# Modulation weights of a diffusion backbone split into two transfers, with both layers written out

## The reference, cut to what matters

```python
mod = jnp.dot(jax.nn.silu(cvec), lp['ada_w']) + lp['ada_b']
sh1, sc1, g1, sh2, sc2, g2 = jnp.split(mod[:, None, :], 6, axis=-1)
h = rmsnorm(x, lp['norm1']) * (1 + sc1) + sh1
proj = jnp.dot(h, lp['w_in'])
q, k, v, xbc, z, dt_raw = jnp.split(proj, SPLITS, axis=-1)
...
x = x + g1 * jnp.dot(jnp.concatenate([attn, ssm], axis=-1), lp['w_out'])
h2 = rmsnorm(x, lp['norm2']) * (1 + sc2) + sh2
x = x + g2 * expert_choice_ffn(h2, lp['w_router'], lp['w_gate'], lp['w_up'], lp['w_down'])
```

## Time and profile before

| | |
|---|---|
| median of 3 runs | 2241.47 us (2241.06 to 2242.45) |
| profiled execution, its own time | 2239.1 us |
| its span, first to last instruction | 2237.4 us |
| PE busy in the span | 1940.9 us (87%) |
| DVE, ACT, POOL busy | 674.2, 306.5, 195.6 us |
| mean granted TensorE clock | 0.914 of full |
| pieces of modulation weights | 16 of 3072 KB, 26.3 us from issue to landing |

### The profile page before, as it was taken

How to read it: one execution, slowest core, us unless ns; L and a number is a source line. 1 busy time by engine, 2 the same in 40 slices (tenths; PEclk the granted TensorE clock), 3 DMA queues, 4 the chain that set the end, 5 groups by cost and what they waited for, 6 DMA issues and landing times.

```text
span 2237.4 us, 36021 instructions
## 1 busy us (share of the span) xinstructions
PE 1940.9 (87%) x15142; PEld 962.6 (43%) x15142; DVE 674.2 (30%) x1486; ACT 306.5 (14%) x684; POOL 195.6 (9%) x266
## 2 busy tenths in 40 slices
PE   2699777996699999999847997779958999999997
PEld 0265465544243443444403744645442443443443
DVE  1130675614211221121212326665251211221121
ACT  1120122301100000000012201233011000000000
POOL 0002220000000100110000022100000100100110
PEclk9899877997799999999968998679968999999998
DMA  9900101033499999999598001012226999999994
GB/s 372 412 1 1 38 1 55 7 154 122 172 384 394 396 407 406 401 409 407 195 394 340 1 0 38 1 55 80 100 104 232 387 406 398 398 409 404 399 405 132
DMA packets 54674, 526.60 MB, mean 235 GB/s; under 512 B 11790, under 2 KB 13438, under 8 KB 25886
## 3 DMA queue, kind: packets, MB, share of 16 engines
q1 hardware_dynamic: 39886, 482.29, 52.9%
q0 software_dynamic: 6336, 21.63, 4.0%
q10 hardware_dynamic: 8384, 21.76, 2.6%
HBM read 503.91 MB, written 24.38 MB: 236 GB/s over the span
## 4 chain that ended last, share of the span: by engine, by line
PE 64%; issue 23%; DMA 6%; POOL 3%; DVE 2%; SPq 1%; ACT 1%; DVEq 0%; POOLq 0%; ACTq 0%
PE PS L469 30%; PE PS L549 13%; DMA arena<-ada_w 6%; PE PS L493 5%; PE PS L495 5%; PE PS L498 4%; PE PS L795 1%; PE PS L479 1%; PE PS L457 1%; PE PS L443 1%; PE PS L519 1%; POOL RB L1536 1%; POOL RB L1545 1%; PE PS L499 1%; SPq L369 1%
## 5 line engine op out<-in xcount | busy, mean ns | idle before, releaser
L469 PE MATMUL PS<-arena,xe 128*32 128x512 f32 x6144 | 674.1, 599 | 4.0 <-DVE xe L1108 4.0
L469 PEld LDWEIGHTS PS<-arena,xe 128*32 128x32 f32 x6144 | 196.8, 111 | 457.7 <-issue 457.7
L493 PE MATMUL PS<-arena,hdT 128*32 128x512 f32 x1536 | 268.3, 599 | 3.8 <-DVE RA L1132 1.9
L495 PE MATMUL PS<-arena,hdT 128*32 128x256 f32 x1024 | 266.2, 383 | 0.0
L1119 DVE TENSOR_TENSOR RA<-RA,PS 96x512 f32<-96x512 f32 (+2 forms) x96 | 63.2, 684 | 649.7 <-ACT RA L864 646.9
L549 PE MATMUL PS<-arena,RB 128*128 128x512 f32 (+2 forms) x640 | 190.1, 456 | 0.0
L498 PE MATMUL PS<-arena,hdT 128*32 128x256 f32 x1536 | 156.6, 381 | 0.0
L499 PE MATMUL PS<-arena,hdT 128*32 128x256 f32 x512 | 153.2, 381 | 0.0
L549 PEld LDWEIGHTS PS<-arena,RB 128*128 128x128 f32 x640 | 108.9, 191 | 79.7 <-issue 75.6
L784 PE MATMUL PS<-arena,RB 128*128 128x512 f32 x320 | 137.8, 593 | 1.7 <-DVE RB L1357 1.7
L519 PE MATMUL PS<-arena,silc 128*2 128x512 f32 x384 | 70.4, 891 | 79.2 <-DMA arena<-ada_w 79.2
(11 more groups left out here) (243 smaller groups left out, 1892.6 us busy)
## 6 DMA issues: line engine op xcount, KB each, us to landing
arena<-w_exp SPq DMA_DIRECT2D x192, 2048.0 KB, 13.3
arena<-ada_w SPq DMA_DIRECT2D x16, 3072.0 KB, 26.3
arena<-w_in SPq DMA_DIRECT2D x4, 4128.0 KB, 21.5
arena<-w_out SPq DMA_DIRECT2D x2, 4096.0 KB, 24.6
RA<-x_res ACTq DMA_DIRECT2D x2, 2560.0 KB, 19.2
RC<-x_res ACTq DMA_DIRECT2D x2, 2560.0 KB, 9.0
x_res<-RC ACTq DMA_DIRECT2D x10, 512.0 KB, 2.6
normed_rows<-RA ACTq DMA_DIRECT2D x10, 512.0 KB, 2.6
```

What stands on the lines that cost most here:

```text
L469: last = mm(PS[GRP * q:GRP * (q + 1), c * 512:(c + 1) * 512], xe[:, k, GRP * grp:GRP * (grp + 1)], w[:, col_, :], start=(k == 0), stop=(k ...
L493: mm(PS[GRP * q:GRP * (q + 1), 1536:2048], tok(q), w[:, 0:512], start=first, **flags)
L495: mm(PS[96:P, 1536 + grp * REST:1536 + (grp + 1) * REST], tok(grp), w[:, MAIN:D], start=first and grp == 0, **flags)
```

## The change

- `ada_w` is passed as two arrays: `ada_first`, the columns of the first two rows of modulation (8.4 MB a layer), and `ada_rest`, the other four (16.8 MB).
- `ada_first` has a buffer of its own, `ada1`. In layer 0 it is the first large transfer; for layer 1 SP issues it in layer 0, ahead of the last expert's `down_parts`, together with the vectors, caches and states.
- `ada_rest` goes in 8 pieces of 2.1 MB through two slots at the end of `arena`, and PE multiplies a piece after every third group of the projection (`rest_of_modulation`). Its sums need two PSUM banks, so the projection cycles through 6 banks and `tokx` through two pairs.
- The second part's strips go into `mrows2`, which lies in `arena` where `w_in` was, so its clearing (`G.memset` on POOL) waits for the projection's last group; copies, transposes and `amp2` follow in the scan's preparation.
- `w_in` of layer 1 is issued as soon as expert weights leave its place; `w_out` after the last piece of `ada_rest`.
- x of layer 0 comes from the inputs, not from `x_res`; the copies into `x_res` are issued later.
- `each_layer` is gone: both layers are written out in the programs, with constants where registers held the wait values. The inner loops over experts stay.

```diff
@@ SP @@
+            def first_modulation(l):
+                for i in range(4):
+                    sp.dma_start(ada1[:, 2 * i:2 * i + 2, :],
+                                 row(ada_first, l)[:, 2 * i * P:(2 * i + 2) * P, :].rearrange("a (k p) n -> p (a k) n", p=P)
+                                 ).then_inc(ada_in[i].sem, 16)
...
+            vectors(0)
+            first_modulation(0)
+            for l in range(LAYERS):
                 for hlf in range(2):
-                    sp.wait_ge(ada_used.sem, ada_used.at(l, 6 + hlf))
+                    if l:
+                        sp.wait_ge(gu_used.sem, gu_used.at(l, 0))
+                        if hlf:
+                            sp.wait_ge(dn_used.sem, dn_used.at(l, -1))
...
+                for c in range(KD):
+                    if c >= 2:
+                        sp.wait_ge(ada2_used.sem, ada2_used.at(l, c - 1))
+                    elif l:
+                        sp.wait_ge(dn_used.sem, dn_used.at(l, 0))
+                    sp.dma_start(ada2[:, c % 2, :], row(ada_rest, l)[:, c * P:(c + 1) * P, :].rearrange("a p n -> (a p) n")
+                                 ).then_inc(ada2_in[c % 2].sem, 16)
...
+                if l + 1 < LAYERS:
+                    sp.wait_ge(stored.sem, stored.at(l, 2 * NT))
+                    sp.wait_ge(col_rdy.sem, col_rdy.at(l, 1))
+                    vectors(l + 1)
+                    first_modulation(l + 1)
+                    caches(l + 1)
                 down_parts(l * EXP + EXP - 1)
@@ PE @@
-                    if n >= 8:
-                        pe.wait_ge(ip_ev.sem, ip_ev.at(l, n - 7))
+                    if n >= 6:
+                        pe.wait_ge(ip_ev.sem, ip_ev.at(l, n - 5))
...
                     n += 1
+                    if n % 3 == 0 and n <= 3 * KD:
+                        rest_of_modulation(n // 3 - 1)
+
+                def rest_of_modulation(c):
+
+                    pe.wait_ge(ada2_in[c % 2].sem, ada2_in[c % 2].at(l, c // 2 + 1))
+                    for b in range(2):
+                        for q in range(4):
+                            last = mm(PS[32 * q:32 * q + 2, (6 + b) * 512:(7 + b) * 512], silc[:, c, :],
+                                      ada2[:, c % 2, (4 * b + q) * 512:(4 * b + q + 1) * 512],
+                                      start=(c == 0), stop=(c == KD - 1), skip_group_check=True)
+                    last.then_inc(ada2_used.sem, 1)
...
+                pe.wait_ge(rows_act2.sem, rows_act2.at(l, 1))
+                pe.wait_ge(rows_dve2.sem, rows_dve2.at(l, 1))
+                for b in range(2):
+                    for i in range(4):
+                        o = (6 + b) * 512 + i * P
+                        last = nc.tensor.transpose(PS[:, o:o + P], mrows2[:, b, i * P:(i + 1) * P], ident[:, :])
+                last.then_inc(mod_ps2.sem, 1)
                 pe.wait_ge(tok_ev.sem, tok_ev.at(l, NT))
+                pe.wait_ge(mod_rdy2.sem, mod_rdy2.at(l, 1))
@@ POOL @@
                 TT(RA[:, 2560:3200].rearrange("p (t c) -> p t c", t=NT), kv_t[:, :, 0:P], kv_t[:, :, 0:P], ALU.mult).then_inc(qs_rdy.sem, 1)
+                pool.wait_ge(ip_ps.sem, ip_ps.at(l, 27))
+                G.memset(mrows2, 0.0).then_inc(rows0_2.sem, 1)
                 pool.wait_ge(hsu_rdy.sem, hsu_rdy.at(l, 1))
                 TT(hs[:, :, :].rearrange("p t h -> p (t h)"), hs[:, :, :].rearrange("p t h -> p (t h)"), mhalf[:, :], ALU.pow).then_inc(hrs_rdy.sem, 1)
```

More of the change, by code:

```diff
@@ L55, in conv_cols, with build @@
     return slice(a, a + P)
-def build(nc, x_prompt, x_sample, cache_k, cache_v, state, vrows, bparams, rope, ada_w, w_in, w_out,
+def build(nc, x_prompt, x_sample, cache_k, cache_v, state, vrows, bparams, rope, ada_first, ada_rest, w_in, w_out,
           w_router, w_exp, x_res, new_k, new_v, new_h):
@@ L147, in build @@
         optmp = RF[:, 0:D]
-        mrows = RF[:, D:D + 1536].rearrange("p (b c) -> p b c", b=3)
+        mrows = RF[:, 2520:3032]
+        mrows2 = arena[:, 4096:5120].rearrange("p (b c) -> p b c", b=2)
+        ada2 = arena[:, KD * IN_DIM:].rearrange("p (i n) -> p i n", i=2)
         hprev = RF[:, 0:2048].rearrange("p (s r c) -> p s r c", s=4, r=2)
@@ L216, in build @@
         wr_in = Signal("wr_in", 1, 16)
-        ada_in = [Signal(f"ada_in{i}", 2, 16) for i in range(4)]
+        ada_in = [Signal(f"ada_in{i}", 1, 16) for i in range(4)]
+        ada2_in = [Signal(f"ada2_in{i}", 4, 16) for i in range(2)]
         win_in = [Signal(f"win_in{i}", 1, 16) for i in range(2)]
@@ L367, in _ @@
                             h = g * GQ + 2 * m
-                            src = row(state)[:, r, h:h + 2].rearrange("a h p n -> (a h p) n")
+                            src = row(state, l)[:, r, h:h + 2].rearrange("a h p n -> (a h p) n")
                             sp.dma_start(hst[:, r, m, g * HD:(g + 1) * HD], src).then_inc(h0_in.sem, 16)
-                for c in range(8):
-                    i = c % 4
-                    if c < 4:
-                        sp.wait_ge(dn_used.sem, dn_used.at(l, 0))
-                    else:
-                        sp.wait_ge(ada_used.sem, ada_used.at(l, c - 3))
-                    sp.dma_start(arena[:, i * 6144:(i + 1) * 6144],
-                                 row(ada_w)[:, c * P:(c + 1) * P, :].rearrange("a p n -> (a p) n")
-                                 ).then_inc(ada_in[i].sem, 16)
+            vectors(0)
@@ L949, in _ @@
                     act.wait_ge(tok_ps.sem, tok_ps.at(l, t + 1))
-                    b = 2 + 2 * (t % 3)
+                    b = 2 + 2 * (t % 2)
                     A(tokx[:, t, :], PS[:, b * 512:b * 512 + 640], ACT.Copy).then_inc(tok_ev.sem, 1)
+                act.wait_ge(rows0_2.sem, rows0_2.at(l, 1))
+                act.wait_ge(ada2_used.sem, ada2_used.at(l, KD))
+                for q in (0, 1):
+                    last = A(mrows2[32 * q:32 * q + 2, :, :], PS[32 * q:32 * q + 2, 3072:4096].rearrange("p (b c) -> p b c", b=2), ACT.Copy)
+                last.then_inc(rows_act2.sem, 1)
                 for t in range(NT):
@@ L1144, in _ @@
             dve.wait_ge(dve_consts, 4)
-            dve.wait_ge(rope_in, 16)
             dve.wait_ge(pool_consts, 8)
-            with each_layer(dve) as l:
+            for l in range(LAYERS):
                 chain.start(l)
@@ L1264, in _ @@
                                 ALU.mult).then_inc(wend_rdy.sem, 1)
+                dve.wait_ge(rows0_2.sem, rows0_2.at(l, 1))
+                dve.wait_ge(ada2_used.sem, ada2_used.at(l, KD))
+                for q in (2, 3):
+                    ins = V.tensor_copy(mrows2[32 * q:32 * q + 2, :, :], PS[32 * q:32 * q + 2, 3072:4096].rearrange("p (b c) -> p b c", b=2))
+                ins.then_inc(rows_dve2.sem, 1)
+                dve.wait_ge(mod_ps2.sem, mod_ps2.at(l, 1))
+                modulation(1, bank(6))
+                link(modulation(2, bank(7)))
+                also(mod_rdy2, V.scalar_tensor_tensor(amp2[:, :, :], mod[:, 32:40, :], 1.0,
+                                                      vp[:, R_N2:R_N2 + 8].unsqueeze(2).broadcast_to([P, 8, 2]), ALU.add, ALU.mult), l, 1)
                 dve.wait_ge(h0_ps.sem, h0_ps.at(l, 1))
@@ L1517, in land @@
                 TT(pgate[:, 1:2], pgate[:, 1:2], pgate[:, 1:2], ALU.add).then_inc(landed.sem, 1)
-            with each_layer(pool) as l:
+            for l in range(LAYERS):
                 for t in range(NT):
@@ L1635 @@
         "rope": rope_table(),
-        "ada_w": a["ada_w"], "w_in": a["w_in"], "w_out": by_pairs(a["w_out"]), "w_router": a["w_router"],
+        "ada_first": a["ada_w"][..., 0:2 * D], "ada_rest": a["ada_w"][..., 2 * D:], "w_in": a["w_in"], "w_out": by_pairs(a["w_out"]), "w_router": a["w_router"],
         "w_exp": expert_slabs(a["w_gate"], a["w_up"], a["w_down"]),
```

144 lines of the change are left out of this document (76 added, 68 removed).

## The result

The changed kernel takes 2248.2 us (median of 11 runs, 2244.15 to 2258.74) where the kernel before takes 2239.5 in the same comparison (11 runs). The ratio is 1.0048, with a 95% interval of 1.003 to 1.0067: slower by 7 to 15 us, where I had forecast 3 less. The profiled execution of the changed kernel was the slowest of the 11 (2258.74).

A forecast was written before the change was run, and what follows sets the result against it. Weights wait for bandwidth first, and PE works with an idle memory later. Terms -55 - 40 + 29.4 + 61.2 + 1.6 = -2.8 us from a 2241.47 median gave 2238.7, stated as 2238.5; 8-in-10 range 2228 to 2249.

The forecast's parts named there:

- Layer 0's start: Start of layer 0: first projection matmul at 45.9 us instead of 101.3, by transfers and x's path alike; gain taken as 55.
- if the clock in the projection is below 1.0: Sign of being wrong: the projection was expected to take 147 to 162 us a layer at clock 1.0.
- The boundary: Layer 0 to layer 1: early loads fill idle transfers, last `down` loses 5.5 us, projection starts at about 1171; gain 40.
- the soft number: Layer 1's load of x: its share of bandwidth beside weights, a fifth to half, changing the time by at most 2 us.
- The chain behind x: Layer 1, from x's landing to the projection: normalizing, copies, transposes and the rest as in layer 0, 20.9 us.
- The products: Projection: eight pieces of 16 records at 1.84 us each, all on PE's path, 14.7 us a layer, 29.4 in all.
- The wait on POOL: End of projection: POOL's power on `hs` waits behind clearing `mrows2`, uncovered, 30.6 us a layer, 61.2 for both.
- The second part's end: Before the scan: copies, transposes, bias and `amp2` delay the fourth state group by 0.8 us a layer, 1.6 in all.
- written out, it runs faster: Rival, both layers: register instructions between linked DVE operations go away, about 6 us, perhaps as much in waits; about 2232; chance 0.15.
- the narrow products cool PE: Rival, projection: two-row products lower PE's clock, 2.3 us a piece, 37 us for sixteen, 2275 us; chance 0.06.
- the order on POOL is covered: Rival, end of projection: the 61 us on POOL are not paid, 2177 us; chance 0.04.
- The boundary is worse: Rival: down parts, scatter and x queue longer, or layer 0's x lands late; 5 to 12 us more, 2244 to 2251; chance 0.14.

The follow-up runs named there:

- the second profile: The changed kernel as it is, profiled again: 2251.0 us, span 2248.9 us, scans 76.8 and 71.4 us.
- the fastest variant: Changed kernel with POOL's power ahead of the clearing, half of `ada_first` ahead of the last down parts, `w_in` issued after x landed: 2167.1 us, ratio 0.9688.
- the second profile of the kernel before: The kernel before as it is, profiled again: 2235.0 us, scans 71.9 and 72.3 us.
- the 22 scans: Scans of both layers in 11 profiles of the changed kernel and its variants: 13 took 76.0 to 78.8 us, the others 70.6 to 72.6.

## Why the prediction was wrong

By its own steps:

- **Layer 0's start**, 45.9 forecast, 49.1 measured. The path of x had slack: x landed at 19.1 us where I had put 25, and the first matmul could run at 42.89. `w_in` was late: 49.3 forecast for the whole, 52.76 measured. The first 5 us moved only 127 GB/s, about what the 3 us for issue and landing had booked, and from 5 us on the transfers were at 0.95 or more. What I had missed is that the loads of one queue overlap: the first packets of `ada_rest`, issued behind `w_in` on the same queue, start at 39.9 us, and the last one of `w_in` ends at 52.3. By then 20.6 MB had moved where I had counted 19.6, which is 2.4 us at 423 GB/s. PE's wait then cost what the forecast had at nothing: the 40 records behind it take 15.11 us, at a mean granted clock of 0.82, where the same ones take 12.1 of layer 1's 15.76 for 48 (15.76 - 3.67). The sign "if the clock in the projection is below 1.0" came true for these 15 us. Together 3.2 + 3 us; the mechanism held, and the term for the bytes ahead of `w_in`'s end was mis-sized.
- **The boundary**, a gain of 40 forecast, 33.5 measured. This step failed in its reasoning. "The last expert's two down parts queue behind on the same queue" was right and costs 5.9 us (5.5 booked). What I hadn't seen is that SP itself stands at its issues: with that, the last `down` ends 10.6 us later than before, counted from the last transposes of `hid`. The scatter gave a little back (8.7 us for 10.1), so x was issued 3.6 us later than forecast. And "all of it together, so x has landed at 1149.5 at the latest" took the sum of bytes as the bound. It is not: x's 2.6 MB take 8.4 us alone and 17 to 26 beside `w_in` and `ada_rest`, and holding 8.45 MB of weights back brings the start forward. In the changed kernel x took 3 us longer than booked. I had noted that x's share was "the soft number" and then let the sum of bytes carry it. One of my own signs of being wrong came true here: layer 0 ended 4.5 us later than before, and x landed at 1160.69, so at 1156.2 in the times of the kernel before, where 1150 was the limit.
- **The chain behind x**, 20.9 forecast, 21.0 measured (1160.69 to 1181.71).
- **The products**, 1.84 a piece forecast; 1.90 by the row, 1.92 by doubling them (1.72 in the rows of the doubled ones). Right.
- **The wait on POOL**, 30.6 a layer forecast, 30.4 measured by taking it away. Right.
- **The second part's end**, 0.8 a layer forecast, 0.9 and -0.1 measured. Right in what it looked at. What it left out is that the same step turns spread state pieces into one dense one, and that the scan behind it then often runs at a lower granted clock: 4.6 us in the two scans of the second profile, 7.6 in those of the first. This term was missing altogether. In the kernel before, one changed wait takes both scans from 71.8 to 78.5 us, so the pattern can cause it. It doesn't do so each time, and what decides between the two outcomes is not shown. What it costs in the end is shown for the kernel before (24 us with the bunching) and not for the fastest variant.
- The rivals "written out, it runs faster", "the narrow products cool PE" and "the order on POOL is covered" are refuted. "The boundary is worse" described what happened there. Its 2244 to 2251 takes in the measured 2248.2, but by luck: of the 14 us that the span of the second profile is over the forecast, 6.4 lie at the boundary.

So in the second profile the forecast is short by 6.4 us at the boundary, some 6 at the first start, 1 in each projection and 5 through the clock in the scan, with some 4 us less in the expert stretches; neither the 1 in each projection nor the 4 has a run here that explains it. The median of the runs missed by 10 and made a small gain a small loss. The large terms, 61.2 on POOL and 29.4 for the products, held.

The result also hides what the change could be: 86 us were gained at the two starts (52.2 and 33.5), 30 were paid for products and 61 for one order on POOL (58 by the medians). With the order mended, half of `ada_first` and the small loads moved behind the down parts, and x let through first, the change is 3.1% faster than before.

## What to carry to other kernels

When work is moved into idle transfer time, ask for each load on the critical path what will lie beside it, not when the last byte of all is in: a short urgent load beside long rows got a quarter to a third of the bandwidth, and a wait that holds the weights back until it has landed was worth 10 to 20 us. Keep small loads out of the issuing engine's way when something urgent is issued behind them. And a new operation on a helper engine that waits for the end of a stage goes behind everything that doesn't need that end: two lines in the other order were worth 58 us.

## What the runs showed of the hardware that I had not expected

- An engine that issues transfers can stand still at an issue while much is queued ahead of it, however small the load: the eight loads of 32 KB took SP 20.63 us in the changed kernel, and 25.34 and 25.11 in the two kernels with all early loads behind the down parts, against 6.00 in the second profile of the kernel before, where little was queued. Nearly all of it is one issue: in the second profile of the changed kernel the first took 17.22 us and each of the others 0.60 or less. That the queue is full then is my reading; no run here counts its places.
- The loads of one queue overlap: in layer 0 the first packets of `ada_rest` start at 39.9 us, 12 us before the last one of `w_in` ends, though `w_in` was issued ahead of it on the same queue.
- The granted clock of a stretch depends on how the work ahead of it is spread, here worth up to 7 us a scan. State matmuls in pieces with gaps were followed by 16 us at 0.89 to 1.00 in the profiles read for it, the same matmuls in one piece of 5.5 us often by 16 us at 0.50 to 0.55 (not always: 9 of the 22 scans behind a dense piece stayed at 70.6 to 72.6 us, six of them behind a piece that took 6.5 to 6.6 us because more of it ran at 0.50). In the thirteen long scans of those 22 the clock falls 5.3 to 5.8 us into the scan and stays low for 17 us or more; in six of the nine short scans it falls at the scan's start and is back before 4 us. PE was busy for 15.26 of the 16 us in the slow case and 14.22 in the fast one, but got through 69 records instead of 114.
- x's load of 2.6 MB took 8.4 us alone, 13.6 beside the last of `ada_first`, 16.6 beside `ada_rest` alone (in the kernel with doubled products), 18.5 to 25.7 beside `w_in` and `ada_rest`.
